# Second attention stage: heads in pairs, both token tiles at once, worked between the projections; layer norm by token tile

## The reference, cut to what matters

```python
k_sh = (x @ w_k_shared).reshape(B, S, N_DIL_HEADS, HEAD_DIM)     # 12 heads of 64
v_sh = (x @ w_v_shared).reshape(B, S, N_DIL_HEADS, HEAD_DIM)
proj = x @ w_in_b[bl]                                            # 12 + 4 heads of queries
mix = dilated_mixture(q, k_sh, v_sh, slopes).reshape(B, S, DIL_OUT_WIDTH)
mo = memory_attention(qm, mk, mv).reshape(B, S, MEM_WIDTH)       # mk, mv = mem @ w_mem_k/v
att = jnp.concatenate([mix, mo], -1) @ w_out_b[bl]
x = layer_norm(ALPHA * x + att, ln1_g[layer], ln1_b[layer])
```

## Time and profile before

| | us |
|---|---|
| median of 3 runs (2380.8 to 2381.92) | 2381.84 |
| the profiled execution's own time | 2386.17 |
| its span, first to last instruction | 2384.4 |
| PE busy / DVE / ACT | 1894.4 / 812.4 / 415.5 |
| mean granted TensorE clock, share of full speed | 0.877 |

### The profile page before, as it was taken

How to read it: one execution, slowest core, us unless ns; L and a number is a source line. 1 busy time by engine, 2 the same in 40 slices (tenths; PEclk the granted TensorE clock), 3 DMA queues, 4 the chain that set the end, 5 groups by cost and what they waited for, 6 DMA issues and landing times. The chain is left out here.

```text
span 2384.4 us, 22348 instructions
## 1 busy us (share of the span) xinstructions
PE 1894.4 (79%) x8956; PEld 942.3 (40%) x8956; DVE 812.4 (34%) x1889; ACT 415.5 (17%) x975; POOL 287.4 (12%) x280
## 2 busy tenths in 40 slices
PE   6999996865555555579789888897798599888986
PEld 4676874521111111136443333332676343333332
DVE  3735036777777776513120000001114300000002
ACT  2172012221212121112111000000123110000001
POOL 1000013434444444200000000000000000000000
PEclk9999998977787777878789999999885699999998
DMA  5223618999999999875259999996722279999995
GB/s 196 106 106 160 265 56 326 420 421 421 421 421 421 421 419 419 354 273 212 102 243 431 431 430 430 431 431 282 322 114 99 90 324 430 431 430 430 430 430 214
DMA packets 68981, 762.38 MB, mean 320 GB/s; under 512 B 9390, under 2 KB 11153, under 8 KB 19970
## 3 DMA queue, kind: packets, MB, share of 16 engines
q1 hardware_dynamic: 31426, 490.66, 49.0%
q0 software_dynamic: 37440, 270.16, 27.4%
HBM read 759.74 MB, written 1.05 MB: 319 GB/s over the span
## 5 line engine op out<-in xcount | busy, mean ns | idle before, releaser
L1669 PE MATMUL bank<-arena 128*64 128x512 f32 x3072 | 695.9, 610 | 80.9 <-DMA arena<-in_w_up 52.9
L726 PE MATMUL bank<-arena 64*64 64x512 f32 x2048 | 350.2, 843 | 253.6 <-ACT arena L531 246.0
L1669 PEld LDWEIGHTS bank<-arena 128*64 128x64 f32 x3072 | 223.6, 140 | 540.4 <-issue 426.1
L989 DVE CUSTOM_DVE_ANT_0 arena<-arena 128x1024 f32<-128x1024 f32 x256 | 313.6, 1225 | 164.7 <-DMA arena<-in_peer_uv,arena 159.1
L366 POOL DMA_INDIRECT arena<-in_peer_uv,arena x256 | 278.1, 1087 | 708.0 <-DVE arena L972 339.7
L726 PEld LDWEIGHTS bank<-arena 64*64 64x64 f32 x2048 | 100.2, 189 | 496.9 <-ACT arena L531 290.8
L1811 DVE TENSOR_TENSOR arena<-arena,bank 128x512 f32<-128x512 f32 x32 | 22.0, 688 | 708.9 <-PE bank L1669 708.9
L556 PE MATMUL bank<-arena 128*128 128x256 f32 (+1 forms) x704 | 161.4, 391 | 0.6 <-DVE arena L775 0.6
L556 PEld LDWEIGHTS bank<-arena 128*128 128x128 f32 x704 | 135.9, 194 | 27.0 <-issue 2.7
L1575 POOL IOTA arena<- 128x128 f32 x2 | 0.5, 243 | 815.1 <-issue 815.1
L531 ACT ACTIVATE arena<-arena 128x64 f32<-128x64 f32 x256 | 68.1, 336 | 143.8 <-DVE arena L998 131.5
(11 more groups left out here) (326 smaller groups left out, 1617.9 us busy)
## 6 DMA issues: line engine op xcount, KB each, us to landing
arena<-in_w_gate SPq DMA_DIRECT2D x32, 4096.0 KB, 30.3
arena<-in_w_up SPq DMA_DIRECT2D x32, 4096.0 KB, 26.2
arena<-in_w_down SPq DMA_DIRECT2D x32, 4096.0 KB, 31.6
arena<-in_w_in SPq DMA_DIRECT2D x16, 2048.0 KB, 9.1
arena<-in_w_out SPq DMA_DIRECT2D x2, 4096.0 KB, 23.6
arena<-in_wq SPq DMA_DIRECT2D x4, 2048.0 KB, 8.5
arena<-in_rg_out SPq DMA_DIRECT2D x1, 4096.0 KB, 17.8
arena<-in_peer_uv,arena POOLq DMA_INDIRECT x256
```

The lines of the kernel that those rows point to most:

```text
L726: m = pe.matmul(bank[banks[t][half]][to:to + HALF, :], DIAG[lo:lo + HALF, k + j, :], row[lo:lo + HALF, D + half * 512:D + (half + 1) * 512 ...
L989: v.tensor_tensor_reduce(SCR, SLOT[slot_of[j]][:, 0:D], XF[:, u // PH, :], 1.0, 0.0, ALU.mult, ALU.add, DOTS[:, u, k:k + 1]).then_inc(s_do ...
L1669: x = pe.matmul(bank[b][j * C:(j + 1) * C, :], operand[:, c, j * C:(j + 1) * C], RING[s % AHEAD][:, j, c, :], start=(c == 0), stop=(c == D ...
```

## The change

`attention_stage(K, 1)` is no longer called. A function of its own, `dilated_stage`, takes its place, and computes the same.

- Projections run as values first (4 jobs), then keys and queries of a pair of heads in turn (`k`, `q`, six times), then the memory's keys, the last two queries and the memory's values. The number and size of all jobs are unchanged.
- Heads go in pairs, p = 0 to 7. A head's scores of both token tiles lie side by side in one bank (3 blocks of 128 keys, 4 for memory heads), the even head of a pair in one bank and the odd head in another. The scale and bias are one DVE operation a head, and there is one copy `PT` a head. The maxima and exponents stay one for each tile.
- PE's order is `k(p)`, values of pair p-2, scores of pair p-1, `q(p)`, transposes of pair p-1, and so on.
- The first 8 heads' outputs are copied on the way. The mixture of the 12 dilated heads is done on DVE before the memory heads, and the memory heads' outputs are scaled straight into `MIX`. The output product is in two parts, the dilated half before the memory half has been transposed.
- The norm runs one tile after the other, and ACT loads its square root table ahead (`WARM`).
- SP loads `w_v` first, in two halves, then `w_k`, `w_in1` in one piece, the bias and the memory rows. The three early expert tiles are issued when all 22 jobs are done.

```diff
-def attention_stage_1(K):
-    attention_stage(K, 1)
+def dilated_stage(K):
...
+    SCORES, TURNED, VALUES = (2, 3), (4, 5), (6, 7)
+    OUT = ((0, 1), (2, 3))
...
+    JOBS = [("v", 0), ("v", 2), ("v", 1), ("v", 3)]
+    for p in range(DPAIRS):
+        JOBS += [("k", p), ("q", p)]
+    JOBS += [("mk", 0), ("mk", 1), ("q", DPAIRS), ("q", DPAIRS + 1), ("mv", 0), ("mv", 1)]
...
+        @block.sync
+        def _(sp):
...
+            sp.wait_ge(s_pm, len(JOBS))
+            for i in range(MOE_EARLY):
+                moe_load(K, sp, 1, i, 0).then_inc(K.s_moe_w[i], 16)
...
+        @block.scalar
+        def _(act):
...
+            def exps(p):
+                for h in (2 * p, 2 * p + 1):
+                    if h >= 2:
+                        act.wait_ge(s_tm, h - 1)
+                    for t in range(TT):
+                        ks = keys_of(h, t)
+                        act.wait_ge(s_sb, TT * h + t + 1)
+                        a.activation(PB[:, h % 2, ks], SB[:, h % 2, ks], ACT.Exp, bias=NEGM[:, t, h:h + 1],
+                                     accum_out=LSUM[:, t, h:h + 1]).then_inc(s_ex, 1)
...
+            for n in range(VALUE_JOBS + 2):
+                leave(*JOBS[n])
+            for p in range(1, DPAIRS):
+                leave("k", p)
+                exps(p - 1)
+                leave("q", p)
+                turned(p - 1)
+            leave("mk", 0)
+            exps(DPAIRS - 1)
+            leave("mk", 1)
+            turned(DPAIRS - 1)
+            act.wait_ge(s_ex, TT * N_DH)
+            a.activation(lse.rearrange("p (t h) -> p t h", t=TT), LSUM[:, :, 0:N_DH], ACT.Ln).then_inc(s_ln, 1)
+            leave("q", DPAIRS)
+            act.wait_ge(s_lse, 1)
+            a.activation(lex, lex, ACT.Exp).then_inc(s_le, 1)
+            leave("q", DPAIRS + 1)
+            exps(DPAIRS)
+            leave("mv", 0)
+            turned(DPAIRS)
+            exps(DPAIRS + 1)
+            leave("mv", 1)
+            turned(DPAIRS + 1)
+            act.wait_ge(s_zero, 1)
+            a.activation(WARM, WARM, ACT.Sqrt)
...
+        @block.tensor
+        def _(te):
...
+            def scores(p):
+                te.wait_ge(s_pj, job("q", p) + 1)
+                for t in range(TT):
+                    for h in (2 * p, 2 * p + 1):
+                        r = slice(h % 2 * HD, (h % 2 + 1) * HD)
...
+                        m = pe.matmul(bank[SCORES[h % 2]][:, ks], QT[r, p, t * P:(t + 1) * P], keys, start=True, stop=True)
...
+            for n in range(VALUE_JOBS + 2):
+                project(*JOBS[n])
+            for p in range(1, DPAIRS):
+                project("k", p)
+                if p >= 2:
+                    values(p - 2)
+                scores(p - 1)
+                project("q", p)
+                turn(p - 1)
+            project("mk", 0)
+            values(DPAIRS - 2)
+            scores(DPAIRS - 1)
+            project("mk", 1)
+            turn(DPAIRS - 1)
+            project("q", DPAIRS)
+            values(DPAIRS - 1)
+            project("q", DPAIRS + 1)
+            scores(DPAIRS)
+            project("mv", 0)
+            turn(DPAIRS)
+            scores(DPAIRS + 1)
+            project("mv", 1)
+            turn(DPAIRS + 1)
+            values(DPAIRS)
+            mix_turn(0)
+            values(DPAIRS + 1)
...
+        @block.vector
+        def _(ve):
...
+            for p in range(5):
+                highest(p)
+            for t in range(TT):
+                ve.wait_ge(s_vm, 8)
+                v.tensor_copy(OALL[:, t, 0:8, :], head_banks(t, 0, 8)).then_inc(s_oc, 1)
+            highest(5)
...
+            highest(6)
+            highest(7)
...
-STAGES = (front_stage, attention_stage_0, moe_stage_0, attention_stage_1, moe_stage_1)
+STAGES = (front_stage, attention_stage_0, moe_stage_0, dilated_stage, moe_stage_1)
```

285 lines of the change are left out of this document (added).

## The result

| | before | changed |
|---|---|---|
| median, us | 2381.88 | 2325.64 |
| profiled execution, its own time / span | 2386.17 / 2384.4 | 2324.13 / 2322.3 |
| mean granted clock | 0.877 | 0.888 |

The ratio is 0.9758, with an interval from 0.9744 to 0.9771: 56 us less, where 56 were forecast (2325.8). One further execution of the changed kernel, 2611.92 us long at a mean granted clock of 0.712, is left out.

A forecast was written before the change was run, and what follows sets the result against it. The second expert stage is bound by fetches that cannot run ahead, so the attention stage's whole length is on the path. 202.6 - 146.1 - 0.5 = 56 us less gives 2330.2, as median 2325.8; range 2316 to 2340.

The forecast's parts named there:

- six steps: Five key and query steps and the memory's keys step, two projection jobs each: together 59.8 us, done at 96.7.
- delay of the expert stage's first step: Second expert stage: its small transfers queue behind the early tiles, 0.5 us added, bounded by 0 and 5.
- 113 us of slack: Expert tile stream: 48 tiles at 429 GB/s would end at 2241, 113 us before the last tile's 2354.62.
- Values, first keys and queries: Attention stage's first jobs after the first wait: 20.8 + 6.9, and 2.1 for half clock, done at 36.8 us.
- 0.4 us of waits: Waits between TensorE's groups of work in each step, taken as 0.4 us.
- 3.3 us of softmax: A pair's scale, maxima and last exponent on DVE and ACT, 3.3 us, hidden under a projection job of 3.45.
- Rival 2: Softmax not covered: six steps stall 1.5 us each, two memory pairs 2 each, +13, 2339 us; chance 10%.
- staircase of alternating records: Scores of a pair: each record starts with its predecessor's second half, 0.85 us instead of 1.28 serial.
- Last jobs and tail: After the six steps: about 2 us of TensorE stall at the first memory pair; end 8.8 after the last matmul.
- rival 1: Clock sinks in part, between jobs or in small work before the output product: 2330 to 2348 us; chance 12%.
- rival 3: Clock stays at half through the stage: slower by 43 us, 2425; chance 3%.
- rival 4: Gain lost behind the early tiles: second expert stage's start loses 5 to 8 us, 2331 to 2334; chance 5%.

The follow-up runs named there:

- experiment 10: Changed kernel with, in both expert stages, the router waiting only for its own two transfers and the input turned through four banks with four wide copies: 2316.12 us.
- experiment 6: Changed kernel with the three early expert tiles issued in the second expert stage, behind its small transfers: 2327.46 us.
- experiment 8: Changed kernel with the first value job waiting for both halves of the value weights: 2328.00 us.
- experiment 4: Changed kernel with a pair's scores ordered head, then tile, instead of tile, then head: 2326.07 us.
- experiment 5: Changed kernel with the values of an earlier pair between the scores of a pair's two heads, in five steps: 2334.12 us.
- experiment 7: Changed kernel with the norm of both token tiles together and without the early square root table load: 2326.82 us.
- experiment 1: Changed kernel with all 22 projection jobs first, then the eight pairs of heads: 2355.72 us.
- experiment 2: Changed kernel with all projections first and four idle matmuls of 256 columns after each pair's scores: 2359.88 us.
- experiment 3: Changed kernel with all projections first and eleven idle matmuls in the one long wait before the last pair's scores: 2357.44 us.

## Why the prediction was right

Point by point, in us from the stage's start, forecast and measured:

| | forecast | measured |
|---|---|---|
| first projection | 7.0 | 7.5 |
| first keys and queries done | 36.8 | 38.0 |
| a step with values | 10.2 | 9.90 |
| six steps done | 96.7 | 96.0 |
| last job done | 116.8 | 115.8 |
| output product begins | 122.8 | 121.3 |
| barrier | 146.1 | 144.9 |
| delay of the expert stage's first step | 0.5 | 0.8 |

(38.0 is 1714.67 less one job, less the start; 96.0 is the end of the transposes that start at 1768.59.)

- *What bounds.* The end moved with the expert stage's first step. That step begins between 1843.4 (experiment 10) and 1914.4 (before), and from there to the end of the span it is 470.0 to 471.5 us in every profile but one. The one is experiment 6, 473.4. So the claim holds as long as the early tiles are fetched ahead. The 113 us of slack that I worked out for the whole stream were no measure of this: with a ring of four, 31 us of later fetching already cost 3.
- *Start.* On the path as said (experiment 8). The half clock at the start cost more than the 2.1 us of the step "Values, first keys and queries": seven jobs of 31.15 us at full clock took 33.99, so 2.8.
- *Steps.* Transposes 0.65 and values 1.38 came as priced. The 0.4 us of waits assumed a step hardly exist, and the 3.3 us of softmax under a job of 3.45 held: no row of a dilated step shows a wait. Rival 2 is refuted.
- *Scores.* 0.86 for 0.85, the right size on a wrong mechanism, so by luck. I had assumed a staircase of alternating records. Experiments 4 and 5 show that two heads run side by side in full, whatever their order within the group, and that 0.2 us a group goes on top. What the 0.2 are is not shown. The Trainium skill ("TensorE: Matmul & The Clock Gate", Part 3) says that matmuls in distinct row groups run concurrently. This agrees with 0.84 for one head and 0.86 for two.
- *Last jobs and tail.* 0.72 us of stall where I had about 2: the table loads of Ln and Exp lay under jobs. The norm's end came 8.6 after the last product matmul, for 8.8.
- *Clock.* 1.00 through the main part and the tail, so rival 1's risk and rival 3 did not come. The rows spoke for it, and the Trainium skill's page ("TensorE: Matmul & The Clock Gate", Part 4) only for a risk. Where transposes stand alone, the trace does not bear the page out. In experiment 7's profile the clock was 1.00 from 1678.6 to 1682.0 behind 16 transposes with idle time on both sides. How thin the ground is, experiments 1 to 3 tell: in the same small operations without jobs between them the clock fell to 0.50 at least twice each.
- *The size of the parts.* Of the 57.7 us of stage, 25.4 are had without interleaving (202.6 to 177.2) and 32.3 by it, about half of these from covered waits (13.4, and the 1.2 for the second bank) and half from the clock (the other 15.3, and 2.1). Of the 25.4, 23.6 lie between the first scores and the output product, where TensorE is busy for 24.8 us less, 1.7 behind that, and nothing before.
- *Chances.* Of rival 4 there may be a trace, the 0.8 us of the last row, but the queue is not shown as its cause. The router matmuls start 7.8 to 8.3 us into the expert stage in the five kernels whose early tiles land just before (the changed one, experiments 4, 5, 7 and 8), and 7.6 to 8.0 in the four whose tiles had long landed (before, experiments 1 to 3).
- *Luck in the sum.* The first keys and queries came 1.2 us late and the six steps took 1.8 us less, so errors of opposite sign met. The median lies within 0.2 us of the forecast, where the executions differ by over 3 among themselves. That closeness says nothing of the working. The rows of the table do, none of them off by more than 1.5.

Not tried: pairing alone, in the old loop by tile and with the old mixture. The 23.6 us stand for all of these together.

## What to carry to other kernels

Small dependent work (scores, softmax, transposes) is worth putting between independent dense jobs: here the jobs covered 13 us of waits and kept the clock, which was worth as much again. Matmuls without use as filler made the kernel no faster: spread over the pairs they cost 4.9 us of stage, and in the one long wait they gave back 2.4. When the next stage is bound by its fetches through a ring, ask when its first step begins. All that stands before that step is on the path, and a wait on four transfers where two are needed cost 6.6 us over two stages.

## What the runs showed of the hardware that was not expected

- Two matmuls of 64 rows in different halves of the array cost together what one does, 0.86 against 0.84 us, in alternating order and head by head.
- The granted clock rose in experiment 1 with nothing on PE but scores, transposes and values. It was 0.53 over 1770 to 1780, with PE busy 10.0 of 10 us, and 1.00 over 1780 to 1790, with PE busy 7.0 of 10. In the loop before it stood at 0.50 with PE busy 10.0 of 10. The busy share of a stretch does not tell its clock.
- Turning the input without a stop made the matmuls behind it faster, 4.67 for 7.01 us, beyond the wait that it saved. Their granted clock was 0.78 instead of 0.50, and in the other expert stage they took 4.37. What raised it, the transposes without stops ahead of them or something else, no run tells apart.
